# Turning the feed-forward's product with VectorE squares and GpSimd transfers in a two-block transformer kernel

## The chip, the cores and the metric

One core of one Trainium2 chip runs the whole program. The metric is the device time of one execution in microseconds (us), the median of three runs. TensorE multiplies matrices, VectorE and ScalarE work on tiles, GpSimd (POOL in the profile) does small arithmetic and issues transfers, SyncE (SP) issues the loads of the weights.

## The reference, cut to what matters

The reference passes 256 tokens of width 2048 through two blocks. The change is in the feed-forward at the end of the first one:

```python
def swiglu(h, w_in, w_down):            # h: (1, 256, 2048)
    g, u = jnp.split(h @ w_in, 2, axis=-1)   # each (1, 256, 5632)
    return (jax.nn.silu(g) * u) @ w_down     # (1, 256, 2048)
...
    x = x + gate_f * swiglu(h, ffn_w_in[l], ffn_w_down[l])
```

All is float32. The product `silu(g) * u` comes out of TensorE with the tokens on the partitions, and has to have its features on the partitions before it can be the stationary operand of the multiplication by `w_down`. Turning it is what the change is about.

## The kernel before, in words

**Precision.** A float32 product is made of three products of a cheaper type: every operand x is split into `hi` (ScalarE writes a rounded copy) and `lo` (VectorE writes x - hi), and hi*hi, hi*lo and lo*hi are summed in PSUM. Weights and activations are both cut so.

**Units.** Work is a list of chunks. A *gemm chunk* is two k-tiles of 128 rows and 512 columns of a weight, 512 KB. SyncE loads it into one of five `raw` slots (`NRAW`, line 813), ScalarE writes `whi`, VectorE writes `wlo` (the `prep` functions; four slots each, `NW`), and TensorE runs its `unit`: 2 k-tiles x 2 token tiles x 3 products = 12 matmuls of 512 columns. An *ada chunk* also uses a `raw` slot, but is multiplied and added on VectorE alone (`acc`, line 1890) and gives TensorE nothing to do. `prep` of a gemm chunk on ScalarE waits until the unit four gemm chunks earlier is done; a `unit` waits for both `hi` and `lo` of its chunk; SyncE loads into a slot when both are done with the chunk before.

**Order.** `make_timeline` writes one list of parts, and every engine runs its share of that list in order. For each chunk it appends the `prep` of the chunk `LOOK` = 3 chunks further on (ada chunks count), then the `unit` (nothing for an ada chunk), then, after a job's last unit, its `evac`, and then lets every active side stage make one `step()`. So a side stage advances once per chunk, ada chunks included.

**The feed-forward.** 5632 hidden features are 11 blocks j of 512. For each, job `fg` j (8 units) and job `fu` j (8 units); ScalarE evacuates `fg` as silu into `sl` (two buffers, `SL`), VectorE evacuates `fu` by multiplying into the same `sl` (two operations of 128x512). Blocks 0 to 5 are followed by four `dn` (0, .) jobs of 12 units, blocks 6 to 10 by four `dn` (1, .) jobs of 10 units. Ada chunks are mixed into the units of blocks 0 to 4 (3 in 7), and none later.

**The turning before.** After `evac` of `fu` j the stage `fx` j is launched (`stage_steps`). Its steps 2 and 3 are `fx_T`: on TensorE four transposes of 128x128 (`quad`, `tr`, line 833) into a PSUM bank `tp`, on ScalarE the copy of the bank to `ah` (128x512), on VectorE `al` = bank - `ah` (`lo_of`). Step 0 is made in the same round as the evacuation, and each later chunk gives one step.

With the parts of the side stages left out, the list around block 0 is: prep `fg`1.1, unit `fu`0.7, **evac `fu`0**, (step 0), prep `fg`1.2, unit `fg`1.0, (step 1), prep `fg`1.3, unit `fg`1.1, (step 2), prep of an ada chunk, (step 3), prep `fg`1.4, unit `fg`1.2, (step 4), prep `fg`1.5, unit `fg`1.3. Here `fg`1.5 is chunk 5 of job `fg` 1. Step 4 lies between prep 4 and prep 5 of the next job for each of the blocks 0 to 4; what follows it is

| block | between step 4 and prep 5 | 
|---|---|
| 0, 4 | nothing |
| 1, 3 | prep of one ada chunk |
| 2 | prep of one ada chunk, then two `ada_add` (VectorE, 1x512) |

For blocks 5 to 10 no ada chunk is near, and step 4 lies between prep 6 and prep 7 of the next job.

**GpSimd** takes the -0.5 powers of the norms, sets some tiles to zero, and issues a few transfers: `brow` for the ada jobs, `xr`, `gfb`, and in the second block `xg` (`lru_b`, line 2664), six transfers from SBUF to SBUF between partitions, one after the other.

Of the kernel before, what the change touches and what calls it, by code (L numbers as in the profile page):

```python
# [16 lines left out]
P = 128  # L17
# [285 lines left out]
def stage_steps(sid):  # L303
# [3 lines left out]
    def step(*parts, need=()):  # L307
        return (list(parts), list(need))
# [51 lines left out]
        return steps  # L360
    if kind == "fx":
        (j,) = args
        return [idle, idle, step(("fx_T", (j, 0), 1)), step(("fx_T", (j, 1), 1))]
    if kind == "hx":
        (j,) = args
        return [idle, step(("hx_T", (2 * j,), 1)), step(("hx_T", (2 * j + 1,), 1)), idle, step(("lf_g", (j,), 0)), step(("lf_sq", (j,), 0))]
# [50 lines left out]
def make_timeline(jobs, units, chunks):  # L417
# [48 lines left out]
    def stat_need(job, k):  # L466
        s = job["stat"]
        if s == "h":
            return [("fnorm", k // 4)]
        if s == "hf":  # L470
            return [("ffn", k // 2 * 2 + 1)]
        if s in ("lq", "lk"):
            return [("lat", s[1], 3 + k // 2)]
        if s == "ot":
            return [("pair", k // 2)]
        if s == "mt":
            return [("mt", k // 4, 3 + k % 4 // 2)]
        if s == "a":
            return [("fx", 6 * job["args"][0] + k // 4, 2 + k % 4 // 2)]
        if s == "h0":  # L480
            return [("hx", k // 4, 1 + k % 4 // 2)]
        if s == "h1":
            return [("lend", 0, k // 2)]
        if s == "mx":
            l = job["args"][0]
            if k < 6:
                return [("ret", l, k % 2, 12 + k // 2)]
            return [("diff", l, 10 * (k - 6) + 9)] if k < 10 else [("lg", l, (k - 10) // 3)]
        return []
# [86 lines left out]
def program(nc, ctx, I, CST, LVL, MSK, out):  # L576
    def sem(name):
        return ctx.enter_context(nc.semaphore(name))
# [12 lines left out]
        sem(n) for n in ("d_c", "d_x", "d_first", "d_lvl", "d_gk", "d_wa", "d_tab"))  # L591
    d_rowl, d_xr, d_gfb, d_gp, d_out = sem("d_rowl"), sems("d_xr", 2), sem("d_gfb"), sem("d_gp"), sem("d_out")
    d_xg = sem("d_xg")

    hi_done, lo_done, mm_done, mm_half, ada_dve = (sem(n) for n in ("hi_done", "lo_done", "mm_done", "mm_half", "ada_dve"))
    ada_sum = sem("ada_sum")
# [78 lines left out]
    def w1(name, kb, shape, dt=F32):  # L675
        return place(name, wk + int(kb * KB), shape, dt)
# [116 lines left out]
    def first_use(*name):  # L793
        return uses[name][0]
# [31 lines left out]
    def pe_program(e):  # L826
# [24 lines left out]
        def result_dve(*name):  # L851

            w.wait_ge(gp_dve[job_of[name]["no"] % 2], at("gpd", *name))

        def quad(bk, src, n=2):

            for a in range(n):
                for t in range(2):
                    last = tr(bk[:, (2 * a + t) * P:(2 * a + t + 1) * P], src(a, t))
            return last  # L860
# [180 lines left out]
            w.wait_ge(xnf_done, 2 * pair + 2)  # L1041
            quad(bk, lambda a, t: XN[:, t, (2 * pair + a) * P:(2 * pair + a + 1) * P]).then_inc(tp_full[u.b], 1)

        def fx_T(us, j, h):
            (u,) = us
            bk = empty(u)
            result_dve("fu", j)
            quad(bk, lambda a, t: SL[j % 2][:, t, (2 * h + a) * P:(2 * h + a + 1) * P]).then_inc(tp_full[u.b], 1)

        def x_T(u, pair):  # L1050
            bk = empty(u)
            quad(bk, lambda a, t: X[:, t, (2 * pair + a) * P:(2 * pair + a + 1) * P]).then_inc(tp_full[u.b], 1)
# [117 lines left out]
        def stationary(job, k):  # L1170

            s = job["stat"]
            if s in ("h", "hf"):
                w.wait_ge(h_hi, at("h", s, k // 2))
                w.wait_ge(h_lo, at("h", s, k // 2))
                return HH[:, k, :], HL[:, k, :]
            if s in ("h0", "h1"):
                u = first_use("hx_T" if s == "h0" else "le_T", k // 2)
                taken_act(u)
                taken_dve(u)  # L1180
                return HH[:, k, :], HL[:, k, :]
            if s == "og":
                u, (hi, lo), i = first_use("gla_og", k // 2 * 2), (OGH, OGL), k
            elif s in ("lq", "lk"):
                u, (hi, lo), i = first_use("lat_T", s[1], k // 2 * 2), LAT[s[1]], k
            elif s == "ot":
                u, (hi, lo), i = first_use("pr_av", k // 2), OT[k // 8], k % 8
            elif s == "mt":
                u, (hi, lo), i = first_use("mt_T", k // 4, k % 4 // 2), MT[k // 8], k % 8
            elif s == "a":  # L1190
                u, (hi, lo), i = first_use("fx_T", 6 * job["args"][0] + k // 4, k % 4 // 2), (AH, AL), k
            else:
                l = job["args"][0]
                if k >= 10:
                    w.wait_ge(mxg_hi, at("mxg", l, k - 10))
                    w.wait_ge(mxg_lo, at("mxg", l, k - 10))
                    return MXH[:, k, :], MXL[:, k, :]
                u, (hi, lo), i = first_use("rt_T", l, k) if k < 6 else first_use("df_X", l, k - 6), (MXH, MXL), k
            taken_act(u)
            taken_dve(u)  # L1200
            return hi[:, i, :], lo[:, i, :]

        def unit(us, n):
# [34 lines left out]
            else:  # L1238

                split = job["name"] in HALVES and ci == len(job["chunks"]) - 1  # L1240
                for kk, t in ((0, 0), (1, 0), (0, 1), (1, 1)) if split else ((0, 0), (0, 1), (1, 0), (1, 1)):
# [6 lines left out]
                    if split and (kk, t) == (1, 0):  # L1248
# [2 lines left out]

        parts = dict(rows=rows, warm=warm, ada_mod=ada_mod, ada_out=ada_out, fn_T=fn_T, gk_la=gk_la, gk_kr=gk_kr, gk_krt=gk_krt,
                     gla_sum=gla_sum, gla_sc=gla_sc, gla_av=gla_av, gla_og=gla_og, lat_T=lat_T, pr_qn=pr_qn, pr_kn=pr_kn, pr_rr=pr_rr, pr_sc=pr_sc,
                     pr_pt=pr_pt, pr_av=pr_av, mt_T=mt_T, f_T=f_T, fx_T=fx_T, hx_T=hx_T, le_T=le_T, le_y=le_y, lx_T=lx_T, lg_T=lg_T, lru_g=lru_g, rp_T=rp_T, rt_S=rt_S,
                     rt_V=rt_V, rt_T=rt_T, df_S=df_S, df_T=df_T, df_V=df_V, df_X=df_X, unit=unit)
        for name, args in line:
            if name in parts:
# [3 lines left out]
    def act_program(e):  # L1261
# [10 lines left out]
        def copy(o, i, scale=None):  # L1272
            return fn(o, i, ACT.Copy) if scale is None else fn(o, i, ACT.Identity, scale=scale)

        def full(u):
            w.wait_ge(tp_full[u.b], u.r + 1)
            return TP[u.b]
# [280 lines left out]
        def f_hi(us, pair):  # L1558
            norm_hi(first_use("f_T", pair), pair, hraw2, "hf")

        def fx_T(us, j, h):
            (u,) = us
            k = 4 * (j % 6) + 2 * h
            bk = full(u)
            if j >= 6:
                w.wait_ge(mm_done, job_of["dn", 0, 3]["chunks"][-1]["w"] + 1)
            copy(AH[:, k:k + 2, :], tok_pairs(bk[:, :])).then_inc(tp_act[u.b], 1)
            note(tp_act[u.b], "tpa", *u)

        def hx_T(us, pair):  # L1570
            w.wait_ge(d_fp, 1)
# [163 lines left out]
        def evac(us, no):  # L1735
# [20 lines left out]
            elif kind == "fg":  # L1756
                i = args[0]
                if i >= 2:
                    read(first_use("fx_T", i - 2, 1))
                for n in range(2):  # L1760
                    fn(SL[i % 2][:, n, :], ps[n][:, :], ACT.Silu).then_inc(gp_act[g], 1)
            elif kind == "v":
# [85 lines left out]
        def after_dve(job):  # L1848
# [11 lines left out]
            if kind == "dn" and args[0] == 1:  # L1860
                ss, j = scol(8, "dn_ss"), args[1]
                for n in range(2):
                    w.wait_ge(x3_done, at("x3", 1, j) - 1 + n)
                    if j or n:
# [3 lines left out]

        parts = dict(rows=rows, x_sq=x_sq, x_norm=x_norm, prep=prep, ada_out=ada_out, fn_T=fn_T, fn_hi=fn_hi, t_sin=t_sin,
                     t_lexp=t_lexp, t_cexp=t_cexp, t_cln=t_cln, gk_la=gk_la, gk_ln=gk_ln, gk_kr=gk_kr, gk_krt=gk_krt, gla_sum=gla_sum, gla_exp=gla_exp,  # L1870
                     gla_av=gla_av, gla_og=gla_og, lat_T=lat_T, pr_qn=pr_qn, pr_kn=pr_kn, pr_rr=pr_rr, pr_sc=pr_sc, pr_pt=pr_pt, pr_av=pr_av, mt_T=mt_T, f_T=f_T, fx_T=fx_T,
                     f_hi=f_hi, hx_T=hx_T, le_T=le_T, lf_sq=lf_sq, lf_x=lf_x, le_sq=le_sq, le_y=le_y, lx_T=lx_T, lru_g=lru_g, lru_e=lru_e, lru_a=lru_a, lru_b=lru_b, lg_T=lg_T, rp_T=rp_T,
                     rt_V=rt_V, rt_T=rt_T, df_S=df_S, df_T=df_T, df_V=df_V, df_X=df_X, evac=evac)
        for name, args in line:
# [4 lines left out]
    def dve_program(e):  # L1879
# [356 lines left out]
            kt = slice(k % 8, k % 8 + 2)  # L2236
            lo_of(u, MT[k // 8][1][:, kt, :], MT[k // 8][0][:, kt, :], tok_pairs(full(u)[:, :]))

        def fx_T(us, j, h):
            (u,) = us  # L2240
            k = 4 * (j % 6) + 2 * h
            if j >= 6:
                w.wait_ge(mm_done, job_of["dn", 0, 3]["chunks"][-1]["w"] + 1)
            lo_of(u, AL[:, k:k + 2, :], AH[:, k:k + 2, :], tok_pairs(full(u)[:, :]))

        def f_rn(us):
            w.wait_ge(ss_done, at("ss", "xo", 3, 1))
# [241 lines left out]
        def evac(us, no):  # L2489
# [86 lines left out]
            elif kind == "w2":  # L2576
# [3 lines left out]
                for n in range(2):  # L2580
# [4 lines left out]
        parts = dict(x_ss=x_ss, prep=prep, ada_mod=ada_mod, ada_add=ada_add, ada_out=ada_out, fn_hi=fn_hi, t_ang=t_ang, t_sin=t_sin,  # L2585
                     t_cos=t_cos, t_lam=t_lam, t_lfin=t_lfin, t_cfin=t_cfin, gk_la=gk_la, gk_sub=gk_sub, gk_rope=gk_rope, gla_z=gla_z, gla_diff=gla_diff, gla_qk=gla_qk,
                     gla_sc=gla_sc, gla_av=gla_av, gla_og=gla_og, lat_T=lat_T, pr_rope=pr_rope, pr_sc=pr_sc, pr_nrm=pr_nrm, pr_av=pr_av, mt_T=mt_T,
                     f_rn=f_rn, f_sc=f_sc, f_hi=f_hi, fx_T=fx_T, hx_T=hx_T, le_T=le_T, lf_rn=lf_rn, lf_g=lf_g, ls_rn=ls_rn, ls_rs=ls_rs, lx_T=lx_T, lx_conv=lx_conv, lru_e=lru_e, lru_a=lru_a,
                     lru_b=lru_b, lg_T=lg_T, rp_r=rp_r, rt_S=rt_S, rt_n=rt_n, rt_s=rt_s, rt_M=rt_M, rt_T=rt_T, df_S=df_S, df_W=df_W, df_V=df_V, df_X=df_X,
                     le_rn=le_rn, le_y=le_y, le_add=le_add, evac=evac)  # L2590
        for name, args in line:
# [4 lines left out]
    def pool_program(e):  # L2596
# [51 lines left out]
        def f_gfb(us):  # L2648
            w.wait_ge(h_lo, at("h", "hf", 7))
            e.dma_start(GFB[:, :], I["final_norm_g"].partition_broadcast(P)).then_inc(d_gfb, 16)  # L2650

        def lf_rn(us):
            power(scol(2, "lf_rs"), "lf")

# [26 lines left out]
        def evac(us, no):  # L2681
# [3 lines left out]
            if kind == "xo":  # L2685
                j = args[0]
                w.wait_ge(m_done, 8)
                if j >= 2:
                    w.wait_ge(x2_done, 2 * (j - 1))
                e.dma_start(XR[j % 2][:, :, :], x_cols[:, :, j, :]).then_inc(d_xr[j % 2], 16)  # L2690

        parts = dict(prep=prep, x_ss=x_ss, gla_loads=gla_loads, gk_krt=gk_krt, rp_T=rp_T, gla_av=gla_av, f_rn=f_rn, f_gfb=f_gfb, lf_rn=lf_rn, ls_rn=ls_rn, lru_b=lru_b, rt_n=rt_n, df_V=df_V,
                     rt_gp=rt_gp, le_rn=le_rn, evac=evac)
        for name, args in line:
            if name in parts:
# [58 lines left out]
```

## Time and profile before

| what | value |
|---|---|
| median of 3 runs | 2645.58 us (2645.3 to 2647.14) |
| the profiled execution | 2647.02 us, its span 2645.2 us |
| granted TensorE clock, mean | 0.994 |
| PE busy | 2556.9 us, 97% of the span |
| VectorE busy | 1699.3 us, 64% |
| ScalarE busy | 1282.6 us, 48% |
| GpSimd busy | 63.3 us, 2% |
| feed-forward's blocks | about 1082 us to 1700 us of the span |

The span is what the profiler sees between the first and the last instruction; the time of the execution has 1.8 us more around it. Busy time of an engine is the union of its instructions. Matmuls are pipelined: one of 512 columns is shown with 389 ns, but the next starts 0.227 us after it, so the pitch of TensorE is read from the starts and from the chain of waits, not from the durations.

### The profile page before, as it was taken

The numbers are of one execution on the slowest core, as the hardware profiler recorded it, in microseconds if no ns is written. First come the engines' busy times: TensorE is split into PE (matmuls) and PEld (weight loads), VectorE is DVE, ScalarE is ACT, GpSimd is POOL, SyncE is SP. The second block draws the span as 40 slices with busy tenths as digits, with TensorE's granted clock in tenths as the row PEclk, the third lists the DMA queues.
The fourth block names the chain that finished last, engine by engine and source line by source line (L and its number), as shares of the span: only waits on it lengthen the run. The fifth ranks groups of instructions, "written<-read, shape, count | busy, mean of one in ns | idle before, by whom it ended". The sixth has DMA issues, their size and how long they took to land.

```text
span 2645.2 us, 33987 instructions
## 1 busy us (share of the span) xinstructions
PE 2556.9 (97%) x12327; PEld 2147.6 (81%) x12327; DVE 1699.3 (64%) x2194; ACT 1282.6 (48%) x1824; POOL 63.3 (2%) x102
## 2 busy tenths in 40 slices
PE   3889999999999999999999999999999999999999
PEld 3888887888887887788888888888888887988887
DVE  5887776776676755566655545565666655676664
ACT  3345455444555444544443444455755545565553
POOL 0000000000000000000000000000000100010000
PEclk9999999999999999999999999999999999999999
DMA  9984665888675765687756666556665465665564
GB/s 363 340 262 152 184 207 183 286 308 269 205 251 192 237 205 180 192 281 252 269 190 192 191 191 190 183 186 182 182 188 175 136 216 148 187 187 176 150 200 135
DMA packets 279921, 555.73 MB, mean 210 GB/s; under 512 B 24287, under 2 KB 45101, under 8 KB 279117
## 3 DMA queue, kind: packets, MB, share of 16 engines
q1 hardware_dynamic: 274048, 541.79, 64.6%
q0 software_dynamic: 3040, 8.69, 1.0%
q10 hardware_dynamic: 2668, 3.09, 0.3%
q8 instruction: 100, 1.64, 0.3%
q14 instruction: 65, 0.52, 0.1%
HBM read 549.83 MB, written 2.10 MB: 209 GB/s over the span
## 4 chain that ended last, share of the span: by engine, by line
PE 90%; DVE 4%; ACT 2%; issue 1%; DMA 1%; SPq 0%; POOL 0%; DVEq 0%; ACTq 0%
PE gp L830 83%; PE tp L830 5%; PE tp L833 2%; DMA raw_first<-in_ada_w_dram 1%; DVE wlo L1884 1%; ACT whi L1270 1%; DVE acc L1890 1%; DVE xs L1884 0%; ACT hraw L1270 0%; SPq L813 0%; DVE stat L2208 0%; ACT sx L1270 0%; DVE sx L1884 0%; DVE yd L1884 0%; ACT h L1270 0%
## 5 line engine op out<-in xcount | busy, mean ns | idle before, releaser
L1884 DVE TENSOR_TENSOR wlo<-raw,whi 128x1024 fp32r<-128x1024 f32 (+1 forms) x830 | 986.1, 1197 | 699.7 <-ACT whi L1270 697.1
L830 PE MATMUL gp<-whi,h 128*128 128x512 f32 (+1 forms) x4352 | 1373.2, 389 | 11.5 <-DVE h L1884 5.5
L1270 ACT ACTIVATE whi<-raw 128x1024 fp32r<-128x1024 f32 (+1 forms) x830 | 851.5, 1037 | 666.6 <-PE gp L830 537.3
L830 PEld LDWEIGHTS gp<-whi,h 128*128 128x128 f32 x4352 | 816.4, 188 | 171.5 <-issue 19.6
L830 PE MATMUL gp<-wlo,h 128*128 128x512 f32 (+1 forms) x2176 | 835.6, 384 | 0.0
L830 PEld LDWEIGHTS gp<-wlo,h 128*128 128x128 f32 x2176 | 410.4, 189 | 72.8 <-issue 1.7
L1890 DVE SCALAR_TENSOR_TENSOR acc<-raw,cact,acc 128x1024 f32<-128x1024 f32 x149 | 190.6, 1279 | 7.7 <-DMA raw<-in_ada_w_dram 7.0
L830 PE MATMUL gp<-whi,ah 128*128 128x512 f32 x352 | 138.0, 392 | 0.0
L830 PE MATMUL gp<-whi,al 128*128 128x512 f32 x352 | 137.1, 390 | 0.0
L830 PE MATMUL gp<-wlo,ah 128*128 128x512 f32 x352 | 137.0, 389 | 0.0
L830 PE MATMUL gp<-h,whi 128*128 128x256 f32 (+1 forms) x528 | 107.2, 300 | 20.7 <-ACT whi L1270 10.7
L830 PEld LDWEIGHTS gp<-h,whi 128*128 128x128 f32 (+1 forms) x528 | 88.5, 202 | 25.5 <-issue 15.9
L830 PE MATMUL gp<-whi,mxh 128*128 128x512 f32 x256 | 99.8, 390 | 0.0
L830 PE MATMUL gp<-whi,mxl 128*128 128x512 f32 x256 | 99.6, 389 | 0.0
L830 PE MATMUL gp<-wlo,mxh 128*128 128x512 f32 x256 | 99.6, 389 | 0.0
L830 PE MATMUL gp<-h,wlo 128*128 128x256 f32 (+1 forms) x272 | 79.8, 293 | 0.0
L830 PEld LDWEIGHTS gp<-whi,al 128*128 128x128 f32 x352 | 66.1, 188 | 13.9
L830 PEld LDWEIGHTS gp<-wlo,ah 128*128 128x128 f32 x352 | 66.1, 188 | 13.4
L830 PEld LDWEIGHTS gp<-whi,ah 128*128 128x128 f32 x352 | 66.1, 188 | 13.5
L2603 POOL TENSOR_TENSOR stat<-stat,cst 128x2 f32<-128x2 f32 (+1 forms) x37 | 30.2, 817 | 1436.9 <-DVE stat L1887 1436.8
L1270 ACT ACT_TABLE_LOAD x44 | 56.5, 1283 | 6.1 <-issue 2.8
L830 PEld LDWEIGHTS gp<-wlo,mxh 128*128 128x128 f32 x256 | 48.1, 188 | 10.0
(331 smaller groups left out, 2594.2 us busy)
## 6 DMA issues: line engine op xcount, KB each, us to landing
raw<-in_w_in_dram SPq DMA_DIRECT2D x310, 512.0 KB, 4.3
raw<-in_ffn_w_in_dram SPq DMA_DIRECT2D x176, 512.0 KB, 4.5
raw<-in_ada_w_dram SPq DMA_DIRECT2D x158, 512.0 KB, 5.0
raw<-in_w_out_dram SPq DMA_DIRECT2D x96, 512.0 KB, 4.4
raw<-in_ffn_w_down_dram SPq DMA_DIRECT2D x88, 512.0 KB, 4.4
raw<-in_w_in_dram SPq DMA_DIRECT2D x64, 384.0 KB, 3.5
raw_first<-in_ada_w_dram SPq DMA_DIRECT2D x34, 512.0 KB, 7.5
raw<-in_gla_wo_dram SPq DMA_DIRECT2D x32, 512.0 KB, 5.7
```

The lines of the kernel that those rows point to most:

```text
L830: return e.matmul(o, l, r, start=start, stop=stop)
L833: return e.transpose(o, i, ident[0:n, 0:n])
L1270: return e.activation(o, i, f, **kw)
L1884: return e.tensor_tensor(o, a, b, op)
L1890: return e.scalar_tensor_tensor(out=o, in0=a, scalar=s, in1=b, op0=op0, op1=op1)
L2603: e.tensor_tensor(dst, dst, cst[:, C_HALF:C_HALF + n], ALU.pow).then_inc(pow_out, 1)
```

## The change: what it does

`fx` j gets other steps. Step 0, in the round of the evacuation, is `fx_t`: VectorE transposes the 32x32 squares of `sl` into a new tile `slt` (two instructions, one for each token tile, 128x512 each), and GpSimd, once both are done, issues 16 transfers from SBUF to SBUF, one for each pair of a source quarter and a destination quarter of the partitions (32 partitions, 2x128 elements, 32 KB each), into a new tile `hrx`. Step 4 is `fx_h`: ScalarE waits for all 16, and writes `ah` for four k-tiles (128x1024) from `hrx`; VectorE waits for that and writes `al` = `hrx` - `ah` (128x1024). TensorE has no part in it any more and waits for `a_hi` and `a_lo`. ScalarE's evacuation of `fg` j waits for VectorE's squares of block j - 2 in place of the transposes.

```diff
     if kind == "fx":
         (j,) = args
-        return [idle, idle, step(("fx_T", (j, 0), 1)), step(("fx_T", (j, 1), 1))]
+        return [step(("fx_t", (j,), 0)), idle, idle, idle, step(("fx_h", (j,), 0))]
@@ stat_need
         if s == "a":
-            return [("fx", 6 * job["args"][0] + k // 4, 2 + k % 4 // 2)]
+            return [("fx", 6 * job["args"][0] + k // 4, 4)]
@@
+    SLT, HRX = w1("slt", 64, [2, 512]), w1("hrx", 68, [2, 4, P])
+    def by_quadrant(b):
+        return b.rearrange("p t a (b i) -> p b (t a) i", b=4)
+    def by_block(b, k):
+        return b[:, k:k + 4, :].rearrange("p b (a i) -> p b a i", i=32)
@@ pe_program
-        def fx_T(us, j, h):
-            (u,) = us
-            bk = empty(u)
-            result_dve("fu", j)
-            quad(bk, lambda a, t: SL[j % 2][:, t, (2 * h + a) * P:(2 * h + a + 1) * P]).then_inc(tp_full[u.b], 1)
@@ stationary
             elif s == "a":
-                u, (hi, lo), i = first_use("fx_T", 6 * job["args"][0] + k // 4, k % 4 // 2), (AH, AL), k
+                w.wait_ge(a_hi, 6 * job["args"][0] + k // 4 + 1)
+                w.wait_ge(a_lo, 6 * job["args"][0] + k // 4 + 1)
+                return AH[:, k, :], AL[:, k, :]
@@ act_program
-        def fx_T(us, j, h):
-            (u,) = us
-            k = 4 * (j % 6) + 2 * h
-            bk = full(u)
+        def fx_h(us, j):
+            k = 4 * (j % 6)
+            w.wait_ge(d_fx, 256 * (j + 1))
             if j >= 6:
                 w.wait_ge(mm_done, job_of["dn", 0, 3]["chunks"][-1]["w"] + 1)
-            copy(AH[:, k:k + 2, :], tok_pairs(bk[:, :])).then_inc(tp_act[u.b], 1)
-            note(tp_act[u.b], "tpa", *u)
+            copy(by_block(AH, k), by_quadrant(HRX)).then_inc(a_hi, 1)
@@ act_program, evac
                 if i >= 2:
-                    read(first_use("fx_T", i - 2, 1))
+                    w.wait_ge(fx_turned, 2 * (i - 1))
@@ dve_program
-        def fx_T(us, j, h):
-            (u,) = us
-            k = 4 * (j % 6) + 2 * h
-            if j >= 6:
-                w.wait_ge(mm_done, job_of["dn", 0, 3]["chunks"][-1]["w"] + 1)
-            lo_of(u, AL[:, k:k + 2, :], AH[:, k:k + 2, :], tok_pairs(full(u)[:, :]))
+        def fx_t(us, j):
+            w.wait_ge(gp_dve[job_of["fu", j]["no"] % 2], at("gpd", "fu", j))
+            w.wait_ge(d_fx, 256 * j)
+            for t in range(2):
+                e.transpose(SLT[:, t, :].rearrange("p (q b i) -> p q b i", q=4, b=4),
+                            SL[j % 2][:, t, :].rearrange("p (b q i) -> p q b i", q=4, b=4)).then_inc(fx_turned, 1)
+        def fx_h(us, j):
+            k = 4 * (j % 6)
+            w.wait_ge(a_hi, j + 1)
+            tt(by_block(AL, k), by_quadrant(HRX), by_block(AH, k).bitcast(F32), ALU.subtract).then_inc(a_lo, 1)
@@ pool_program
+        def fx_t(us, j):
+            if j:
+                w.wait_ge(a_lo, j)
+            w.wait_ge(fx_turned, 2 * j + 2)
+            for a in range(4):
+                for q in range(4):
+                    e.dma_start(HRX[32 * q:32 * q + 32, :, a, :], SLT[32 * a:32 * a + 32, :, P * q:P * q + P]).then_inc(d_fx, 16)
```

## Rows read from the trace of the kernel before

**Rows 1.** The page's first part: busy time, share of the span, instructions.

```profile
PE 2556.9 (97%) x12327; PEld 2147.6 (81%) x12327; DVE 1699.3 (64%) x2194; ACT 1282.6 (48%) x1824; POOL 63.3 (2%) x102
```

**Rows 2.** Windows (ada blocks, later blocks): PE, PEld, DVE, ACT, POOL busy, clock, DMA share, GB/s.

```profile
1106.60:1310.00 203.40, 203.40 (x914) 167.79 (x913) 138.14 (x127) 84.44 (x93) 0.96 (x2) 1.00 0.79 268
1506.60:1695.00 188.40, 188.40 (x851) 155.98 (x851) 95.28 (x87) 79.51 (x85) 0.00 (x0) 1.00 0.64 190
```

**Rows 3.** The chain of waits, 1080 to 1350 us: start, us, what.

```profile
1112.18 0.87 PE tp L833 x8
...
1153.88 0.44 PE tp L833 x4
1154.31 2.76 PE gp L830 x12
1157.07 0.44 PE tp L833 x4
```

**Rows 4.** TensorE's transposes that read tile sl, whole run.

```profile
L833 PE MATMUL tp<-cst,sl x88: 270/272/273, 1112.0 to 1694.5; 128*128 128x128 f32 x88
```

**Rows 5.** Timeline of TensorE around block 0's transposes: start, us, instruction.

```profile
1111.56 0.39 PE L830 MATMUL gp<-wlo,h 128*128 128x512 f32 x1
1111.79 0.39 PE L830 MATMUL gp<-whi,h 128*128 128x512 f32 x1
1112.02 1.03 PE L833 MATMUL tp<-cst,sl 128*128 128x128 f32 x8
```

**Rows 6.** Timeline of ScalarE and VectorE, 1100 to 1150 us: idle before, releaser in brackets.

```profile
1101.39 1.06 ACT L1270 ACTIVATE whi<-raw 128x1024 fp32r<-128x1024 f32 x1 [1.66 <-PE gp L830]
...
1106.83 1.06 ACT L1270 ACTIVATE whi<-raw 128x1024 fp32r<-128x1024 f32 x1 [1.66 <-PE gp L830]
...
1102.55 1.23 DVE L1884 TENSOR_TENSOR wlo<-raw,whi 128x1024 fp32r<-128x1024 f32 x1 [1.50 <-ACT whi L1270]
...
1106.77 1.29 DVE L1884 TENSOR_TENSOR sl<-gp,sl 128x512 f32<-128x512 f32 x2 [2.33 <-PE gp L830]
```

**Rows 7.** Groups by form, 1085 to 1790 us: busy us, mean ns of one.

```profile
L1884 DVE TENSOR_TENSOR wlo<-raw,whi 128x1024 fp32r<-128x1024 f32 x253 | 308.3, 1225 | 264.0 <-ACT whi L1270 263.4
L1270 ACT ACTIVATE whi<-raw 128x1024 fp32r<-128x1024 f32 x253 | 266.2, 1059 | 300.3 <-PE gp L830 267.6 <-DMA raw<-in_ffn_w_in_dram 32.7
...
L1890 DVE SCALAR_TENSOR_TENSOR acc<-raw,cact,acc 128x1024 f32<-128x1024 f32 x30 | 38.4, 1279 | 0.3 <-DMA raw<-in_ada_w_dram 0.3
...
L1884 DVE TENSOR_TENSOR acc<-acc,brow 1x512 f32<-1x512 f32 x4 | 2.7, 680 | 0.1
...
L1887 DVE TENSOR_SCALAR acc<-raw,cact 128x1024 f32<-128x1024 f32 x2 | 1.5, 748 | 0.0
```

**Rows 8.** Timeline around GpSimd's six xg transfers, 1901 to 1908 us.

```profile
1900.90 0.66 DVE L2347 TENSOR_TENSOR_SCAN xc<-la,li 96x256 f32<-96x256 f32 x1
...
1901.48 1.20 DVE L1884 TENSOR_TENSOR wlo<-raw,whi 128x1024 fp32r<-128x1024 f32 x1
...
1901.85 3.10 POOL L2664 DMA_DIRECT2D xg<-xc  x6 [84.85 <-DVE xc L2347]
```

**Rows 9.** Tile xg, whole run: issue ns min/median/max; all its transfers to landing.

```profile
L2664 POOL DMA_DIRECT2D xg<-xc x24: 503/519/547, 1901.9 to 2350.8; - x24
...
DMA to landing us min/median/max: 1.7/2.0/4.7
```

**Rows 10.** DMA issues of GpSimd, whole run: KB each, median us to landing.

```profile
xg<-xc POOLq DMA_DIRECT2D x8, 64.0 KB, 2.8
...
xg<-xc POOLq DMA_DIRECT2D x8, 32.0 KB, 2.2
```

**Rows 11.** GpSimd's issues by form, the slowest with 128 partitions in two pieces.

```profile
L2690 POOL DMA_DIRECT2D xr<-in_x_dram x4 | 2.9, 737 | 210.3 <-DVE m L1884 168.0 <-DVE xs L1884 42.3
```

**Rows 12.** DMA queues, 1895 to 1940 us: packets, MB, share of 16 engines.

```profile
q0 software_dynamic: 448, 0.79, 5.9%
```

More of the change, by code:

```diff
@@ L593, in program @@
     d_xg = sem("d_xg")
+    fx_turned, d_fx, a_hi, a_lo = (sem(n) for n in ("fx_turned", "d_fx", "a_hi", "a_lo"))
     hi_done, lo_done, mm_done, mm_half, ada_dve = (sem(n) for n in ("hi_done", "lo_done", "mm_done", "mm_half", "ada_dve"))
@@ L1253, in pe_program @@
                      gla_sum=gla_sum, gla_sc=gla_sc, gla_av=gla_av, gla_og=gla_og, lat_T=lat_T, pr_qn=pr_qn, pr_kn=pr_kn, pr_rr=pr_rr, pr_sc=pr_sc,
-                     pr_pt=pr_pt, pr_av=pr_av, mt_T=mt_T, f_T=f_T, fx_T=fx_T, hx_T=hx_T, le_T=le_T, le_y=le_y, lx_T=lx_T, lg_T=lg_T, lru_g=lru_g, rp_T=rp_T, rt_S=rt_S,
+                     pr_pt=pr_pt, pr_av=pr_av, mt_T=mt_T, f_T=f_T, hx_T=hx_T, le_T=le_T, le_y=le_y, lx_T=lx_T, lg_T=lg_T, lru_g=lru_g, rp_T=rp_T, rt_S=rt_S,
                      rt_V=rt_V, rt_T=rt_T, df_S=df_S, df_T=df_T, df_V=df_V, df_X=df_X, unit=unit)
@@ L1870, in act_program @@
                      t_lexp=t_lexp, t_cexp=t_cexp, t_cln=t_cln, gk_la=gk_la, gk_ln=gk_ln, gk_kr=gk_kr, gk_krt=gk_krt, gla_sum=gla_sum, gla_exp=gla_exp,
-                     gla_av=gla_av, gla_og=gla_og, lat_T=lat_T, pr_qn=pr_qn, pr_kn=pr_kn, pr_rr=pr_rr, pr_sc=pr_sc, pr_pt=pr_pt, pr_av=pr_av, mt_T=mt_T, f_T=f_T, fx_T=fx_T,
+                     gla_av=gla_av, gla_og=gla_og, lat_T=lat_T, pr_qn=pr_qn, pr_kn=pr_kn, pr_rr=pr_rr, pr_sc=pr_sc, pr_pt=pr_pt, pr_av=pr_av, mt_T=mt_T, f_T=f_T, fx_h=fx_h,
                      f_hi=f_hi, hx_T=hx_T, le_T=le_T, lf_sq=lf_sq, lf_x=lf_x, le_sq=le_sq, le_y=le_y, lx_T=lx_T, lru_g=lru_g, lru_e=lru_e, lru_a=lru_a, lru_b=lru_b, lg_T=lg_T, rp_T=rp_T,
@@ L2587, in dve_program @@
                      gla_sc=gla_sc, gla_av=gla_av, gla_og=gla_og, lat_T=lat_T, pr_rope=pr_rope, pr_sc=pr_sc, pr_nrm=pr_nrm, pr_av=pr_av, mt_T=mt_T,
-                     f_rn=f_rn, f_sc=f_sc, f_hi=f_hi, fx_T=fx_T, hx_T=hx_T, le_T=le_T, lf_rn=lf_rn, lf_g=lf_g, ls_rn=ls_rn, ls_rs=ls_rs, lx_T=lx_T, lx_conv=lx_conv, lru_e=lru_e, lru_a=lru_a,
+                     f_rn=f_rn, f_sc=f_sc, f_hi=f_hi, fx_t=fx_t, fx_h=fx_h, hx_T=hx_T, le_T=le_T, lf_rn=lf_rn, lf_g=lf_g, ls_rn=ls_rn, ls_rs=ls_rs, lx_T=lx_T, lx_conv=lx_conv, lru_e=lru_e, lru_a=lru_a,
                      lru_b=lru_b, lg_T=lg_T, rp_r=rp_r, rt_S=rt_S, rt_n=rt_n, rt_s=rt_s, rt_M=rt_M, rt_T=rt_T, df_S=df_S, df_W=df_W, df_V=df_V, df_X=df_X,
@@ L2690, in evac @@
                 e.dma_start(XR[j % 2][:, :, :], x_cols[:, :, j, :]).then_inc(d_xr[j % 2], 16)
-        parts = dict(prep=prep, x_ss=x_ss, gla_loads=gla_loads, gk_krt=gk_krt, rp_T=rp_T, gla_av=gla_av, f_rn=f_rn, f_gfb=f_gfb, lf_rn=lf_rn, ls_rn=ls_rn, lru_b=lru_b, rt_n=rt_n, df_V=df_V,
+        parts = dict(prep=prep, x_ss=x_ss, gla_loads=gla_loads, gk_krt=gk_krt, rp_T=rp_T, gla_av=gla_av, f_rn=f_rn, f_gfb=f_gfb, fx_t=fx_t, lf_rn=lf_rn, ls_rn=ls_rn, lru_b=lru_b, rt_n=rt_n, df_V=df_V,
                      rt_gp=rt_gp, le_rn=le_rn, evac=evac)
```

## The prediction

> **What bounds the kernel now.** I read first the page's busy times: TensorE works 97% of the span, VectorE 64%, ScalarE 48%, GpSimd 2% [rows 1]. Then the windows: in the blocks of the feed-forward TensorE is busy for the whole window, 203.40 of 203.40 us and 188.40 of 188.40 us, at a granted clock of 1.00 [rows 2]. So each us taken from TensorE there is a us of the kernel, and each us for which it has to wait is one too. Then the chain of waits: it runs through TensorE's matmuls alone, and the transposes stand in it with 0.87 us for eight in a row and 0.44 us for four [rows 3]. That is the price to use. The duration of one transpose, 272 ns [rows 4], would give 24 us for all 88, but they are pipelined, and 0.11 us each is what they hold up. Last, the timelines of ScalarE and VectorE give who waits for whom: in steady state ScalarE writes whi of a chunk right after the unit four before it is done, so cut weights for about three to four units lie ready, and no more.
>
> **What is removed.** 11 blocks x 8 transposes at 0.87 us for eight: 9.6 us, all on the path. Also 22 copies to ah and 22 subtractions to al of 128x512. ScalarE gets 11 copies of 128x1024 in their place, VectorE 11 subtractions and 22 transposes; their sum changes little on engines with a third or half of their time free, so I cost it at nothing by itself. It costs where it stands in the order, which comes next.
>
> **What is added, block by block.** Let T be the start of the first matmul behind fu j. For block 0 two units (24 matmuls at a pitch of 0.227 us, 5.44 us) lie between T and the transposes at 1112.02 us, so T = 1106.58 us [rows 5], and VectorE starts its product at 1106.77 us = T + 0.19 and needs 1.29 us for both halves [rows 6]: T + 1.5.
>
> The squares of 32: the trace of before has no transpose on VectorE. The lower bound is its fastest form, one source at 748 ns for 128x1024, so 0.37 us for 128x512 [rows 7]; the upper one the scan, 0.66 us for 256 columns, so 1.3 us for 512 [rows 8]. I take 0.65 us, that of the product of the same shape just before [rows 6], as one element passes per lane. Two of them: T + 2.8. This sits ahead of the cuts of the next chunks on VectorE; in block 1, with an ada chunk between, wlo of chunk 2 would be done at T + 2.8 + 1.28 + 1.23 = T + 5.3 where TensorE wants it at T + 5.4, so it is just hidden; elsewhere it has at least 1.2 us more.
>
> GpSimd then issues 16 transfers. Between the scan's end at 1901.56 us and the issue of xg at 1901.85 us lie 0.29 us, and six issues take 3.10 us, 0.517 us each [rows 8], with VectorE cutting weights beside them. These are the nearest rows: SBUF to SBUF, 32 to 96 partitions. So the first is issued at T + 3.1 and the last at T + 3.1 + 15 x 0.517 = T + 10.9. A transfer of 32 KB lands 2.2 us after its issue [rows 10]: T + 13.1. The bounds: issue 0.503 us [rows 9] to 0.737 us, the xr transfers, which have two pieces in each partition as the new ones do [rows 11]; landing 1.7 to 4.7 us [rows 9]. Nothing else is queued on GpSimd that anyone waits for in these blocks but two brow rows, and SyncE's queue isn't touched.
>
> ScalarE stands at fx_h until T + 13.1, and behind it in its order are the cuts of the next weights; VectorE stands behind ScalarE, and SyncE's loads behind both. This is the wait that the change adds. The copy of 128x1024 takes 1.06 us: T + 14.2. VectorE starts 0.10 us after ScalarE's end (1102.55 - 1101.39 - 1.06 [rows 6]) and needs 1.23 us for al: T + 15.5, and 1.23 us for wlo of the next chunk, whose whi ScalarE wrote meanwhile [rows 7]: T + 16.7, with some 0.15 us until TensorE starts, T + 16.9.
>
> When does TensorE want that chunk? In blocks 0 to 4 step 4 lies before the cut of chunk 5, since ada chunks have used up part of the look-ahead. Chunks 0 to 4 keep TensorE busy for 60 x 0.227 = 13.6 us, so it stands for 16.9 - 13.6 = 3.3 us. Where an ada chunk comes in between on VectorE (1.28 us), 4.6 us; in block 2 with two adds of 0.68 us besides, 5.9 us [rows 7]. In blocks 5 to 10 step 4 lies before the cut of chunk 7, which is wanted at T + 84 x 0.227 = T + 19.1: the same wait is hidden there, with 2.2 us to spare. The dn jobs want block 5's tiles only ten units on and block 10's eight, well after T + 16.9.
>
> After a stall VectorE has one cut of 1.23 us per 2.72 us of TensorE, and the five raw slots were filled meanwhile, so nothing follows behind it.
>
> **The sum.** Removed 9.6 us. Added 2 x 3.3 + 2 x 4.6 + 5.9 = 21.7 us. Net 12.1 us slower. Against the profiled execution's 2647.02 us that is 2659.1; that one lies 1.4 us above the median of the runs, and from the median, 2645.58 us, it is 2657.7. I take 2658.
>
> The trace has a whole turning of 128x128 on TensorE at 0.11 us on the path [rows 3]. The Trainium skill (VectorE: DVE Perf Modes, The three transpose paths and Rules for kernel authors) gives 390 ns for TensorE's and 311 ns for VectorE's, in bfloat16, says that VectorE turns only squares of 32, and advises TensorE where the result may go to PSUM. By its 390 ns 34 us would be removed, and the sum would be 2633; the rows, which are of this kernel, decide against that figure and make its advice weigh more.
>
> **Rivals.**
> *The wait is covered, and the gain stands: 2636 to 2640 us.* To cover it in every block ScalarE would have to be released at about T + 7.2, 5.9 us earlier (2636 us); with 3.5 us earlier the stalls left are 0, 1.1, 2.4, 1.1 and 0 us, and it is 2640.6. For it: blocks 5 to 10 are covered, and TensorE has no other wait there. Against it: 16 issues in a row take 8.3 us by the six of xg; 3.5 us less asks for issues of 0.28 us each. Chance 0.07. This is the other side of my forecast, and it decides by one thing, the pitch of GpSimd's issues: at 0.36 us each, 2.4 us earlier, the stalls are 0.9 + 2.2 + 3.5 + 2.2 + 0.9 = 9.7 us, and the change is worth nothing.
> *Partly covered: 2641 to 2650 us.* A pitch between 0.3 and 0.4 us, or squares at 0.37 us with landings at 1.7 us and still less before them. The lower ends of all three prices together give 1.3 us less per block, 6.3 us in all, so 2651, just outside. Chance 0.10.
> *The transfers come late, and all eleven blocks stall: 2672 us and more.* With issues at 0.737 us the last goes out 3.3 us later: the five stalls grow by 16.5 us, and blocks 5 to 10 stall by 3.3 - 2.2 = 1.1 us each, 7 us together: 2681 us. With landings of 4.7 us it is 2.5 us each: 12.5 + 2 us, 2672 us. For it: 1024 pieces of 512 bytes in 8 us have to pass beside SyncE's loads, which hold 79% of the transfer engines' time in the first blocks [rows 2]; GpSimd's packets took 0.059 x 16 x 45 us / 448 = 95 ns each [rows 12], an estimate of up to 6 us of all 16 engines for each block. Against it: SyncE's loads stop too while ScalarE waits. Chance 0.14.
>
> **The numbers.** Main case, five stalls and six hidden waits, chance 0.69, its own range 2651 to 2671 (the low ends together; a landing of 4.7 us or squares of 1.3 us, which add 6.5 us, alone). The range of 8 in 10 is 2646 to 2678. About 0.2% is what a measurement of this kernel can tell from no change, that is 2640.3 to 2650.9 us. Faster: the covered case, 0.07. Same: the partly covered one and a little of the main one, 0.12. Slower: the rest, 0.81.
>
> **What the changed profile would show.** No PE MATMUL of tp from sl; in the chain, in their place, pieces of DMA hrx, ScalarE's ah, VectorE's al and wlo, in five places some 45 us apart from 1120 to 1300 us, and none in the blocks after 1320 us. GpSimd's group of hrx with 176 issues near 520 ns, 91 us busy. ScalarE's ah x11 with about 9 us of idle time before each in the first five blocks and about 4 us in the later ones. TensorE's idle time before gp larger by about 22 us, its busy time less by about 10. I am wrong if issues take well under 0.4 us, if TensorE is still busy throughout, if the later blocks stall as well, or if the time between stalls grows beyond 43.5 us of matmuls, which would point to the loads or to VectorE.

## The result, and the profile after

The changed kernel takes 2677.78 us (median of 4 runs, 2676.4 to 2682.55) against 2645.87 us of the kernel before (4 runs): 1.0123 times, 95% interval 1.0109 to 1.0138, or 31.9 us more where 12.1 were forecast. That is just inside the stated range of 2646 to 2678 us, with a loss more than twice the one forecast. The profiled execution took 2682.55 us with a span of 2680.7, so it lies 4.8 us above its median; the rows below are of it.

The page of the changed kernel, its busy times, the part by slices that shows the clock, and three of its groups:

```profile
PE 2558.5 (95%) x12239; PEld 2144.4 (80%) x12239; DVE 1708.3 (64%) x2205; ACT 1279.1 (48%) x1813; POOL 155.8 (6%) x278
...
PEclk9999999999999999999899999999999999999999
...
L840 PE MATMUL gp<-whi,h 128*128 128x512 f32 (+1 forms) x4352 | 1376.5, 391 | 37.1 <-DVE wlo L1888 30.0
...
L2667 POOL DMA_DIRECT2D hrx<-slt x176 | 92.6, 536 | 545.0 <-DVE slt L2247 543.6
...
L1888 DVE TENSOR_TENSOR al<-hrx,ah 128x1024 fp32r<-128x1024 f32 x11 | 13.5, 1225 | 83.2 <-ACT ah L1276 83.2
```

The 88 transposes are gone (12327 - 12239 matmuls [rows 1]), and yet TensorE is busy for 2558.5 us, not less than the 2556.9 before: part of its matmuls ran slower. The windows of the changed kernel over the blocks with ada chunks and over the later ones (columns as in [rows 2]) say where. Those of the kernel before over the same stretches have 262.99 and 394.88 us of work at 1.00:

```profile
1082.00:1345.00 263.00, 232.72 (x977) 188.78 (x976) 153.50 (x142) 94.65 (x99) 44.74 (x85) 0.94 0.71 235
1345.00:1740.00 395.00, 392.50 (x1723) 322.77 (x1721) 205.20 (x190) 162.46 (x164) 50.48 (x96) 1.00 0.65 199
```

30 us without work and a mean clock of 0.94 in the first, 2.5 us without work at 1.00 in the second. The chain of waits around block 0 shows one such place whole (start, us, what):

```profile
1104.93 3.42 PE gp L840 x15
1108.37 1.30 DVE sl L1888 x2
1110.33 0.68 DVE slt L2247
1111.29 7.91 POOL hrx L2667 x15
1119.20 4.76 DMA hrx<-slt
1123.99 1.06 ACT ah L1276
1125.08 0.97 DVE al L1888
1126.22 1.23 DVE wlo L1888
1127.58 2.47 PE gp L840 x5
```

In this block T is 1108.37 - 0.19 = 1108.18 us. GpSimd's first issue is at T + 3.1 and its last at T + 11.0, as forecast (10.9). But that transfer lands 4.76 us later, not 2.2: ScalarE is released at T + 15.8 and TensorE starts at T + 19.4, where T + 13.1 and T + 16.9 stood in the prediction. And what TensorE does then is slow. Its timeline behind the stall, and windows of 2 us there:

```profile
1121.54 0.39 PE L840 MATMUL gp<-whi,h 128*128 128x512 f32 x1
1127.58 0.76 PE L840 MATMUL gp<-whi,h 128*128 128x512 f32 x1 [5.65 <-DVE wlo L1888]
1128.14 0.63 PE L840 MATMUL gp<-wlo,h 128*128 128x512 f32 x1
1128.57 1.05 PE L840 MATMUL gp<-whi,h 128*128 128x512 f32 x2
1129.42 0.63 PE L840 MATMUL gp<-wlo,h 128*128 128x512 f32 x1
```

```profile
1126.00:1128.00 2.00, 0.42 (x1) 0.45 (x2) 2.00 (x3) 2.00 (x3) 0.00 (x0) 0.50 0.00 0
1128.00:1130.00 2.00, 2.00 (x6) 1.52 (x6) 2.00 (x3) 0.83 (x1) 0.00 (x0) 0.50 0.71 195
```

The granted clock is 0.50 (1.2 of 2.4 GHz) after TensorE has stood for more than 5 us, and the starts are 0.43 us apart in place of 0.227. From 1127.58 to 1131.12 us eight starts pass, which take 1.8 us at full clock: 1.7 us lost. The other stalls of the blocks with ada chunks look the same, but for block 2. There TensorE stands ahead of the turning of the ada job's sum, which comes before chunk 5. It starts behind the first of the two adds, and the second add and the cut of chunk 5 (`wlo`) are made while it runs:

```profile
1229.12 1.39 DVE L1888 TENSOR_TENSOR acc<-acc,brow 1x512 f32<-1x512 f32 x2
1230.55 2.36 DVE L1888 TENSOR_TENSOR wlo<-raw,whi 128x1024 fp32r<-128x1024 f32 x2
```

```profile
1229.95 3.72 PE L840 MATMUL tp<-acc,cst 128*128 128x512 f32 x4 [5.67 <-DVE acc L1888]
```

**The account**, by the starts of VectorE's product in sl and of the last yd in the two profiled executions. Before block 0 the changed one is already 1.6 us later, which is no part of the change. Blocks 0 to 4 take 260.86 us against 225.95: 34.9 us more. Of these, 4.4 us were gained by five blocks' transposes; TensorE stood for 5.65 + 5.85 + 5.67 + 6.20 + 5.87 = 29.2 us; the remaining 10.1 us, 2 us a block, are nearly all its slow matmuls. Read from the starts, these cost 1.7 to 2.3 us behind each stall, 9.6 us in all, and each stall is 0.16 us longer than its idle time, since a matmul is shown for longer than the pitch; that makes 30.0 us of standing. From block 5 to the last yd it takes 466.61 us against 468.03, a gain of only 1.4 us. The kernel nowait below, which has no stall, takes 462.23 us for the same, so the six blocks' transposes are worth 5.8 us there; 4.4 us of it went to five stalls of 0.27 to 1.08 us, 3.0 us of idle time and about 0.27 us more for each from start to start. That makes 35.1 of the 35.5 us between the two profiled executions.

### The profile page after: what moved, and what is told of

The parts are those of the page before. It is cut to its first block, busy times and chain, and to the rows that moved or that the text cites. A ratio compares the mean times of both kernels' runs of the same rounds, so it can differ in the third digit from the quotient of the medians.

```text
span 2680.7 us, 33986 instructions
## 1 busy us (share of the span) xinstructions
PE 2558.5 (95%) x12239; PEld 2144.4 (80%) x12239; DVE 1708.3 (64%) x2205; ACT 1279.1 (48%) x1813; POOL 155.8 (6%) x278
## 3 DMA queue, kind: packets, MB, share of 16 engines
q10 hardware_dynamic: 2668, 3.09, 0.3%
q8 instruction: 100, 1.64, 0.2%
## 4 chain that ended last, share of the span: by engine, by line
PE 82%; DVE 6%; DMA 3%; ACT 3%; POOL 3%; issue 2%; SPq 0%; DVEq 0%; ACTq 0%; POOLq 0%
PE gp L840 75%; PE tp L840 5%; POOL hrx L2667 3%; PE tp L843 2%; DVE wlo L1888 2%; DMA hrx<-slt 2%; DMA raw_first<-in_ada_w_dram 1%; ACT whi L1276 1%; DVE acc L1894 1%; ACT ah L1276 0%; DVE xs L1888 0%; ACT hraw L1276 0%; DVE sl L1888 0%; ACT sx L1276 0%; DVE stat L2212 0%
## 5 line engine op out<-in xcount | busy, mean ns | idle before, releaser
L2667 POOL DMA_DIRECT2D hrx<-slt x176 | 92.6, 536 | 545.0 <-DVE slt L2247 543.6
L840 PEld LDWEIGHTS gp<-h,whi 128*128 128x128 f32 (+1 forms) x528 | 88.9, 203 | 25.5 <-issue 15.8
L1888 DVE TENSOR_TENSOR al<-hrx,ah 128x1024 fp32r<-128x1024 f32 x11 | 13.5, 1225 | 83.2 <-ACT ah L1276 83.2
```

The lines of the kernel that those rows point to most:

```text
L840: return e.matmul(o, l, r, start=start, stop=stop)
L1888: return e.tensor_tensor(o, a, b, op)
L2667: e.dma_start(HRX[32 * q:32 * q + 32, :, a, :], SLT[32 * a:32 * a + 32, :, P * q:P * q + P]).then_inc(d_fx, 16)
```

## The experiments

Each kernel ran beside runs of the kernel before on the same chip, and the ratios are against those; their medians were 2643.9 to 2646.4 us.

**1. The wait moved down.** Kernel late8:

```diff
-        return [step(("fx_t", (j,), 0)), idle, idle, idle, step(("fx_h", (j,), 0))]
+        return [step(("fx_t", (j,), 0)), *[idle] * 7, step(("fx_h", (j,), 0))]
...
-            return [("fx", 6 * job["args"][0] + k // 4, 4)]
+            return [("fx", 6 * job["args"][0] + k // 4, 8)]
```

> The changed kernel with fx_h at step 8 in place of step 4, nothing else. Theory 1 (the loss is the wait of ScalarE and VectorE at fx_h, which stands too early in their order): at step 8 the transfers, landed by T + 16, are there when the engines come to fx_h, TensorE never stands for them, its clock stays at 1.00 through the blocks, and the 9.6 us of the transposes are gained: 2636 us, 0.4% under the kernel before. Theory 2 (the transfers' traffic beside the weights' loads, or VectorE's and ScalarE's new work, holds TensorE up wherever fx_h stands): 2655 us or more, with stalls of TensorE left in the blocks with ada chunks.

Measured: 2640.01 us, 0.9976 times the kernel before (0.9965 to 0.9987), where 2636 was expected. 37.8 us of the changed kernel's time lie in where two instructions (ScalarE's ah and VectorE's al, with their waits) stand in the order. Its clock stays at 1.00:

```profile
1082.00:1380.00 298.00, 295.84 (x1295) 242.46 (x1294) 192.23 (x177) 126.12 (x130) 52.46 (x100) 1.00 0.78 259
```

The 4 us missing are three small stalls: 1.64 us in block 1 and 0.50 us in block 2, where ScalarE at fx_h still waits for the transfers (for 5.40 us in block 1), and 1.04 us in block 10, where step 8 comes too late for the first dn (1, .) job, which waits for al.

**2. No wait, with and without the transfers.** In nowait, ah and al read slt:

```diff
-            w.wait_ge(d_fx, 256 * (j + 1))
+            w.wait_ge(fx_turned, 2 * j + 2)
...
-            copy(by_block(AH, k), by_quadrant(HRX)).then_inc(a_hi, 1)
+            copy(by_block(AH, k), by_quadrant(SLT.rearrange("p t (a b) -> p t a b", a=4))).then_inc(a_hi, 1)
```

> The changed kernel with ah and al made from slt, the tile of VectorE's squares, as soon as these are done; the 16 transfers of each block are issued as in the changed kernel, but only the next block's squares wait for them. Leaves out the move between the partition quarters, so ah and al hold other values. Theory 1: without the wait TensorE loses nothing, 2636 us, like the kernel with step 8. Theory 2 (traffic): the transfers still run beside the loads, so it stays at 2650 us or more.

> As the kernel without the wait, and the 176 transfers aren't issued at all. Leaves out the move between the partition quarters. Theory 1: the same as without the wait, 2636 us within 2 us, since the traffic costs nothing by itself. Theory 2 (traffic): it is at least 8 us faster than the kernel that issues them and doesn't wait.

Measured: 2635.33 us (0.9955, 0.9939 to 0.997) with the transfers and 2636.30 us (0.9959, 0.9945 to 0.9972) without them (nodma). As theory 1 has it: 11 x 0.87 = 9.6 us are what the transposes cost on the path, and 5.8 MB of transfers beside the weights cost nothing that can be measured.

**3. TensorE kept at work in the stall.** Kernel fill, in `unit`, ahead of its waits for hi and lo:

```diff
+            if job["kind"] == "fg" and job["args"][0] in (1, 2, 3, 4, 5) and ci == 5:
+                result_dve("fu", job["args"][0] - 1)
+                for _ in range(22):
+                    mm(gp[2 - 2 * g][:, :], HH[:, 0, 0:P], H2[:, 0, :, :].rearrange("p a b -> p (a b)"), True, True)
```

> The changed kernel, and TensorE makes 22 matmuls of 512 columns more, whose results nobody reads, ahead of its wait for chunk 5 of jobs fg 1 to 5, where it stands for about 5.9 us in the changed kernel. They take 5.0 us at 0.227 us each, inside the stall. If the clock's fall to half speed behind each stall is a part of the loss, then the granted clock stays at 1.00 in these blocks and the time falls by 1.7 to 2.5 us for each of five stalls, 8 to 12 us in all: about 2667 us. If the half clock costs nothing (theory 3: the matmuls behind a stall wait for weights anyway), it stays at 2677 us.

Measured: 2677.28 us, no gain in all. In block 2 the stall is at `tp<-acc`, as shown above, ahead of chunk 5; the filling came behind it and was 5 us of path. Blocks 0, 3 and 4, where the clock is 1.00 behind the stall, take 1.5, 1.7 and 2.1 us less than in the changed kernel (49.58, 50.51 and 51.31 us against 51.11, 52.17 and 53.39); block 1, where it fell again, takes 1.1 us more. So fill2 leaves that block out (`in (1, 2, 4, 5)`).

> As the kernel with the 22 matmuls in the stall, but none in block 2, where the stall lies before the ada job's sum and they came behind it, 5.1 us on the path. The clock's part of the loss is then seen in four blocks: at full clock behind the stall each block is about 1.5 to 2 us shorter than in the changed kernel, 2670 us in all. If the half clock costs nothing, 2677 us.

Measured: 2674.96 us, 2.8 us less than the changed kernel and not the 7 expected. Block 0 is the clean case. The timeline of fill2's TensorE there:

```profile
1118.97 5.15 PE L840 MATMUL gp<-h 128*128 128x512 f32 x22
```

```profile
1124.81 0.47 PE L840 MATMUL gp<-whi,h 128*128 128x512 f32 x1 [0.69 <-DVE wlo L1892]
1125.11 0.39 PE L840 MATMUL gp<-wlo,h 128*128 128x512 f32 x1
1125.34 0.63 PE L840 MATMUL gp<-whi,h 128*128 128x512 f32 x2
```

The weights come at T + 19.4 us as in the changed kernel, the clock is full, and from sl of block 0 to that of block 1 it takes 49.47 us against 51.10: 1.6 us back, the 1.7 us read from the starts. That the clock's fall is a cost of its own is shown in that block, and in the three of fill. The other blocks of fill2 gave little or nothing, for two reasons. In blocks 1 and 3 the clock fell in spite of the filling, behind the stalls of 2.49 and 2.08 us that it left, so the expected full clock was had in two blocks of four. And in blocks 1, 3 and 4 ScalarE was released 0.9 to 1.6 us later than in the changed kernel; why is open.

**4. Why the landings take 4.8 us.** In small, at step 4 and with the wait, each transfer moves `0:16` of its 128 columns.

> The changed kernel, with its wait at step 4, but each of the 16 transfers moves 2x16 elements in a partition in place of 2x128 (an eighth of the bytes in as many pieces, 64), and ah and al are made from slt, so they hold other values; the move between the quarters is left out. Theory A (the landings of 4.8 us against the 2.2 us that I took come from the bytes beside the weights' loads): the last transfer lands within 3 us of its issue, at T + 13.5 or so, and the stalls shrink by about 2 us each, 2666 us. Theory B (they come from the number of pieces and transfers, the making of which lags behind the issue on GpSimd or waits its turn behind the loads' large packets): the landing stays above 4 us and the time at 2675 us or more.

Measured: 2670.02 us (1.0096, 1.0082 to 1.0110), between the two. The median landing falls from 4.4 to 3.6 us in blocks 0 to 3, ScalarE is released at T + 13.8 to T + 15.1. So the bytes are 0.8 us of the 2.2 us that the median of 4.4 us lies above the 2.2 us forecast, less than half of it. Two more kernels show the rest. In eight, GpSimd issues only half of the transfers (`for a in range(2)`), and ah and al read slt; in split, all 16 are made, 8 of them issued by ScalarE:

```diff
+        def fx_t(us, j):
+            if j:
+                w.wait_ge(a_lo, j)
+            w.wait_ge(fx_turned, 2 * j + 2)
+            for a in range(2, 4):
+                for q in range(4):
+                    e.dma_start(HRX[32 * q:32 * q + 32, :, a, :], SLT[32 * a:32 * a + 32, :, P * q:P * q + P]).then_inc(d_fy, 16)
```

> The changed kernel, wait at step 4, with 8 of the 16 transfers of each block left out (those from the upper two source quarters), and ah and al made from slt, so they hold other values. Theory 1 (GpSimd's issues, one each 0.53 us, set the release together with the landing of the last): the last issue goes out 8 x 0.53 = 4.2 us earlier, ScalarE is released at about T + 11.5, TensorE stands for about 1.5 us in block 0 and 2 to 3 us in the others with ada chunks, its clock stays at 1.00, blocks 5 to 10 are covered: 5 x 2 to 2.5 us, 2646 us. Theory 2 (the transfer engines are the limit, not the issues): the landings shrink with the number of transfers too, and it is 2640 us or less.

> The changed kernel with the 16 transfers of each block divided between two queues, 8 issued by GpSimd and 8 by ScalarE, at the same places of their orders, the wait still at step 4. Theory 1: the issues go out side by side, ScalarE is released near T + 11.5 as with eight transfers, and the time falls from 2677 to about 2646 us, if ScalarE's eight issues (0.4 to 0.5 us each, as on SyncE) delay its cuts by 4 us that it has. Theory 2 (transfer engines): the landings of the last get longer and it stays above 2660 us.

Measured: eight 2662.19 us (1.0066, 1.0051 to 1.0081), split 2697.00 us (1.0199, 1.0184 to 1.0214). Both miss what was expected, and together they answer the question. The transfers of block 6 in eight (1528.4 to 1534.7 us) and in split (1543.7 to 1550 us), queues first, then the issues with their median us to landing:

```profile
q1 hardware_dynamic: 546, 1.06, 63.7%
q0 software_dynamic: 232, 0.24, 12.2%
...
hrx<-slt POOLq DMA_DIRECT2D x8, 32.0 KB, 3.9
```

```profile
q0 software_dynamic: 256, 0.26, 17.3%
q10 hardware_dynamic: 640, 0.26, 17.0%
q1 hardware_dynamic: 15, 0.03, 1.1%
...
hrx<-slt ACTq DMA_DIRECT2D x8, 32.0 KB, 1.9
hrx<-slt POOLq DMA_DIRECT2D x8, 32.0 KB, 1.8
```

The same 8 issues on GpSimd at the same pitch land after 3.9 us while the weights' loads (q1) hold 63.7% of the transfer engines, and after 1.8 us while they hold 1.1%, though twice as many transfers are under way. So the rest of the landing is time spent behind the weights' loads; a kernel in which only these are held back was not run. The Trainium skill (DMA: Bandwidth & Descriptors, Anatomy of one DMA) has a fixed 2.0 us plus the bytes at 436 GB/s for a transfer issued by GpSimd, an estimate of 2.1 us for 32 KB. The trace is near it where the loads are quiet (1.8 us), and 1.8 to 3.3 us longer beside them (3.9 to 5.4 us).

Why are the loads quiet in split? Because ScalarE is issuing. The rows of its sequencer and of hrx's issues in that block:

```profile
1543.24 5.15 ACTq L1573 DMA_DIRECT2D hrx<-slt  x8
1548.50 3.90 ACT L1276 ACTIVATE whi<-raw 128x1024 fp32r<-128x1024 f32 x4 [9.58 <-issue]
```

Eight issues take it 5.15 us, 0.64 us each, not the 0.4 to 0.5 of my expectation (SyncE's own are 0.34 to 0.37 us in these blocks), after a wait for the squares. For 9.6 us it cuts no weights, so no slot comes free and no load starts, and in all eleven blocks TensorE stands until about T + 10.7: 5.1 us in the first five, 2.4 to 2.7 us in the others. Release near T + 11 was reached and did not help.

In eight the release came at T + 12.0 to 13.0 and TensorE stood for 1.9 to 3.6 us in blocks 0 to 4, with none in the later ones. It took 16 us more than the 2646 expected, though the stalls, 14.1 us in all, are only 2 to 4 us longer than expected. The largest part of the rest is the clock again, which I had put at 1.00. Four of the five windows of 50 us over these blocks have less:

```profile
1100.00:1150.00 50.00, 48.12 (x206) 39.37 (x205) 31.56 (x29) 19.08 (x21) 4.25 (x8) 0.97 0.76 249
...
1200.00:1250.00 50.00, 46.38 (x189) 36.57 (x188) 30.43 (x29) 19.09 (x21) 5.21 (x10) 0.93 0.69 228
```

Blocks 0 to 4 take 22.3 us more here than in the last kernel below, 244.12 against 221.82 us: 14.1 us of standing and 8.2 us that are nearly all slow matmuls. The median of eight lies 3.4 us above its profiled execution; these 3.4 us are not explained.

**5. Only the later blocks moved.** In lateend, `n = 4 if j < 5 else 6` takes the place of the number of the step.

> The changed kernel with fx_h at step 6 in blocks 5 to 10 alone; blocks 0 to 4 keep step 4. The part of the loss that lies in the later blocks: 0.3 to 1.1 us in five of the six by TensorE's waits, 3.0 us in all, so 2674 to 2675 us, and the rest, some 40 us against the version with both moved, lies in the five blocks with ada chunks.

Measured: 2675.86 us (1.0120, 1.0103 to 1.0137), 1.9 us less than the changed kernel, and no stall of TensorE at a cut of weights in blocks 5 to 10. In the profiled executions 39.0 of the 43.5 us between the changed kernel and the next one, from sl of block 0 to the last yd, lie in blocks 0 to 4, and 4.5 us in the later ones.

**6. Each wait where its block bears it.** Kernel best:

```diff
+        n = 10 if j < 5 else 6
+        return [step(("fx_t", (j,), 0)), *[idle] * (n - 1), step(("fx_h", (j,), 0))]
...
+            j = 6 * job["args"][0] + k // 4
+            return [("fx", j, 10 if j < 5 else 6)]
```

> The changed kernel with fx_h at step 10 in blocks 0 to 4 and at step 6 in blocks 5 to 10. Theory 1 (the whole loss is the place of the wait): the two stalls of some 2 us that step 8 left in blocks 1 and 2, and the 1.3 us that it cost in block 10, where the first dn (1, .) job wanted the tiles, are gone: 2636 us, some 4 us under the kernel with step 8 throughout, and no stall of TensorE in the blocks beyond what the evacuations cost before. Theory 2 (the loads are held up by the transfers, so that something stays): 2639 us or more.

Measured: 2633.03 us (5 runs, 2632.42 to 2636.27), 0.9953 times the kernel before (0.994 to 0.9967). From sl of block 0 to the last yd it takes 684.0 us, against 687.8 in late8 and 683.4 in nowait: the wait costs next to nothing now. Its windows over the blocks, then its page's first line:

```profile
1082.00:1330.00 248.00, 247.62 (x1085) 203.26 (x1085) 166.24 (x154) 106.79 (x111) 44.15 (x85) 1.00 0.82 272
1330.00:1700.00 370.00, 370.00 (x1634) 306.39 (x1633) 197.44 (x180) 154.88 (x152) 50.51 (x96) 1.00 0.65 202
```

```profile
PE 2546.2 (97%) x12239; PEld 2138.5 (81%) x12239; DVE 1709.7 (65%) x2205; ACT 1282.9 (49%) x1813; POOL 155.8 (6%) x278
```

TensorE's busy time is 10.7 us under [rows 1], its waiting in 618 us is 0.4 us, and from sl of block 0 to the last yd the profiled execution is 10.0 us shorter than before, where 9.6 was the term for the transposes. The landings are even later here, 5.2 to 5.5 us by the median in blocks 0 to 4, since the loads never pause (q1 at 79.6%), and cost nothing.

## Why the prediction was wrong, point by point

- **The gain, 9.6 us: right in size.** Priced by the chain's 0.44 us for four [rows 3] and not by 272 ns each [rows 4]; the kernels without the wait are 11.1 and 10.1 us below their kernel before, and the last one's blocks are 10.0 us shorter (nowait's 10.5).
- **The mechanism and its place: right.** ScalarE and VectorE stand at fx_h with the next cuts behind them; five stalls where step 4 lies before chunk 5, shown by moving that step alone.
- **The squares, the issues and the cuts: right in size.** 690 ns against 0.65 us, 0.53 against 0.517 us, ah 1.06 and al 1.23 us.
- **The landing: the first wrong term.** "A transfer of 32 KB lands 2.2 us after its issue [rows 10]: T + 13.1." It was 3.2 to 5 us for the last transfer, and ScalarE's release T + 14.8 to T + 16.7. The row was the median over eight transfers of xg from stretches with fewer loads: in that of [rows 12] q1 held 54.6% of the transfer engines, against 68.2% here; [rows 9] had 4.7 us as the longest, and [rows 2] the engines' 79%. I had it as a rival with 0.14, when the loads' share in this very window made it the likelier. It made the idle time 29.2 us in place of 21.7 (30.0 us by the starts) and took the cover from the later blocks, where 2.2 us were said to be spare.
- **Block 2 was right by luck.** 5.9 us were forecast and 5.67 measured. The release was 2.0 us late there as well, but the path behind it was 2.1 us shorter than the sum has it: TensorE waits there for the first add, and not for the second (0.68 us) and the cut of chunk 5 behind it (1.23 us). Over the five blocks the releases were 11.4 us late; this took 2.1 us back, and 0.2 to 0.3 us in each of the others.
- **The clock: the second, and missing altogether.** "So it stands for 16.9 - 13.6 = 3.3 us" counted standing only. After 5 to 6 us of it TensorE ran at 0.50 for the first matmuls, 2 us more per block, 9.6 us in all by the starts. No row of the transposes' surroundings showed it, but the trace of before had a mean of 0.994 and not 1: from 2216 to 2222 us its clock is 0.51, behind stalls of 1.8 and 0.8 us.
- **"Nothing follows behind it": wrong** for that reason; VectorE's cuts did catch up as said. Two of the prediction's signs of being wrong came: the later blocks stall, and from the first stall to the second it takes 45.5 us in place of 43.5. The cause of the longer time was the clock, and not the loads or VectorE as the prediction has it.
- The error of 20 us is thus about 7.5 us of longer stalls, 10.1 us of clock (0.8 us of it the stalls' length that idle time does not show), 3.8 us in the later blocks, and 2.0 us outside the blocks: 23.4 us in the profiled execution, of which 3.6 us are its distance from the median.
- **The rival with late landings** (2672 us and more) is what came, with its reason: SyncE's loads. That its time was reached is luck, though: it had no clock in it, and without the 9.6 us the kernel would be at about 2668 us. Against it stood that the loads stop while ScalarE waits. They do, but the slots still to be filled are loaded during most of the burst: in block 0 the transfer engines are busy for 80% and more from 1113 to 1121 us, and idle only from 1123 us on; q1 held 68.2% over blocks 0 to 3.

## What to carry to other kernels

Work that leaves the bounding engine for a longer path gains only if the wait for its result stands late enough in the order of the engines that feed the bounding one: count the chunks of look-ahead at that place, for each kind of surroundings, not in the steady state. Price a transfer's landing by rows with the same load on the transfer engines as at the place where it will run. And a stall of the bounding matrix engine has a second bill: look at the granted clock behind the next one of the same length.

## What the runs showed of the hardware that was not expected

- Eight SBUF-to-SBUF transfers of 32 KB took ScalarE's sequencer 5.15 us and GpSimd 4.21 us, in block 6 of split.
- Landings of 32 KB in 64 pieces: 1.8 us with the weights' queue at 1.1% of the transfer engines, 3.9 us at 63.7%, 5.4 us at 79.6%; an eighth of the bytes in as many pieces still took 3.6 us at 68.3%.
- The clock fell to 0.50 behind each of the changed kernel's five stalls of 5.65 to 6.20 us, and not behind one of 3.60 us in block 0 of small; yet in eight it was 0.97 over the 50 us that hold one stall of 1.88 us, and in split it fell behind the stall of 2.38 us in block 6 and not behind that of 2.36 us in block 5. The length of the stall alone doesn't say whether it falls, and no run here settles what does.
- VectorE turns the 32x32 squares of a float32 tile of 128x512 in 690 ns, as long as a product of that shape (686 ns).
